# Nine convolution projections of a delta-rule stage as three products of rounded parts, with the weights' rests formed by GpSimd

## The chip, the cores and the metric

The kernel runs on one core of a Trainium2 chip. The metric is the device time of one execution in microseconds; the median of several runs counts. TensorE (PE) multiplies; ScalarE (ACT), VectorE (DVE) and GpSimd (POOL) work elementwise; SyncE (SP) issues nearly all loads.

## The reference

256 tokens of width 1024 go through two stacks of two layers each. The change lies at the seam: the first stack's last residual is normalised, normalised again for the second stack and modulated, and goes into the "gated delta rule" mixer:

```python
h = rmsnorm(x, norm_mix) * (1 + scale) + shift          # [256, 1024], float32
mixed, z, beta_in, a_in, q, k, v = split(h @ hy_w_in)    # first 1536 columns: mixed
mixed = causal_conv_silu(mixed, gdn_conv)                # 4 taps over tokens, then silu
```

The first 1536 columns of the product are twelve tiles of 128 channels, called `("conv", 0)` to `("conv", 11)` in the kernel. Their convolution gives the delta rule's query, key and value. The squares of the first eight tiles are summed per head (l2 norm), and a decay comes from eight further columns, the tile `("ba",)`. After it come four `z` tiles and twelve tiles `mq`, `mk`, `mv` of a second attention.

## The kernel before

Each projection tile is one "unit" of weights, 128x1024 float32 (512 KB), loaded by SP into one of eight slots of `ring` in a fixed order; a slot is loaded again when the unit that used it is done (`unit_done`). Activations are kept turned, channels on partitions, as eight blocks of 128x256 (`hT`, `xT`). PE writes tile t into PSUM bank t mod 3, and may start a tile only when the tile three before it has been evacuated (`evac`).

There are two ways of multiplying. `stream` (line 856) is a plain float32 product, eight matmuls of 256 columns for a unit. `stream_split` (line 878) takes operands rounded to the type float32r: it needs `weight_high` (a rounded copy of the weights in the arena, by ACT, `weights_high`, L1999), `weight_low` (the rest, weights minus rounded weights, written over the slot of the ring, by DVE, `weights_low`, L3054), and the same two parts of the activations (ACT, `rounded_hidden`, L1986; DVE, `split_hidden`, L3067). A unit is then 24 matmuls: rest of weights by rounded activations, rounded weights by rest of activations, rounded by rounded. Before the change the MLP, the first tiles of the first stack and the `pq` tiles of the second go this way; the convolution tiles don't.

`weights_high(label, ahead)` makes the rounded copies up to `ahead` units beyond the label, three unless told otherwise. There are four buffers (`HIGH = 4`), so the copy for a unit waits until the split unit four before it is done.

No engine is reordered at run time: each has its queue as the program writes it. Around the change the queues are these.

- PE: the last `down` tiles (split), the raw tiles `conv` 0 to 2 (L967, made from unnormalised activations), sums for a modulation vector (L1028), then `stream` of `conv` 3 to 11 (L856), `ba` (L852), sums of squares (L1514), four `z` and two `mq` tiles (L856), and then matmuls that wait for DVE (L1520).
- DVE: `two_norms` (the normalisation, `raw_out` of `conv` 0, the scaled activations L2640, `raw_out` of `conv` 1 and 2, a second reciprocal, the rescaling of `xT` L2690), a reduction of the modulation (L3031), and then in `gdn` for each of the twelve tiles one multiply and three multiply-adds (L3106, L3109), four taps of the convolution; after them the small decay operations, four operations L3136 and a large reciprocal (L2628).
- ACT: the root (L1810), the shift of `hT` (L1798), the second root, and then in `gdn` the loop below.
- POOL: idle until the shifted `hT` is there, and then two small loads (L2437) of the decay's inputs into `ab_t`, which lay inside the area of `weight_high`.

The loop on ACT, where `silu(j)` first waits for DVE's taps of tile j:

```python
for j in range(12):
    if j < RAW:                  # RAW = 3; DVE has evacuated these
        by_vector(("conv", j))
    else:
        evac(("conv", j), conv_in[:, j, 3:3 + S])
    if j >= 2:
        silu(j - 2)
```

Of the kernel before, what the change touches and what calls it, by code (L numbers as in the profile page):

```python
# [27 lines left out]
P = 128  # L28
S = 256
# [146 lines left out]
def two_stacks(nc, io, out):  # L176
    ctx = ExitStack()
    with ctx:
# [14 lines left out]
        def rounded(name, over, first, shape):  # L193

            t = nc.alloc_sbuf_tensor_at(name, shape, F32R, offset=address[over] + 4 * first)
            return t[(slice(None),) * len(shape)]
# [173 lines left out]
                tile(("sub", l, j), [unit_of(sk[4 * j:4 * j + 4].rearrange("a n d -> n a d"), P, 4, P)], P)  # L370
            stage_units[l] = len(units)

        IN_PARTS = ("up", "down", "sk", "sr", "sv", "pc", "pq")
        PLAIN = {kind: [(l, j) for l in range(DEPTH) for j in range(RAW)] for kind in ("pq", "up")}
        gate_units, narrow = [], {}
        for l in range(DEPTH):
            for b in (0, 3, 1):
# [23 lines left out]

        def last_in_parts(label):

            for kinds in (("sk", "sr", "sv", "pc"), ("up", "down"), ("pq",)):
                if label[0] in kinds:
                    return [x for x in tiles if x[0] in kinds and x[1] == label[1]][-1]
# [119 lines left out]
        hidden_high = rounded("hidden_high", "arena", 25856, [P, KD, S])  # L526
        first_weight_high = rounded("first_weight_high", "arena", 0, [P, HIGH, 1024])
        first_high, first_low = rounded("first_high", "uT", 0, [P, KD, S]), rounded("first_low", "arena", 30112, [P, KD, S])
        second_low = rounded("second_low", "arena", 27904, [P, KD, S])
        early_high, early_low = rounded("early_high", "arena", 21760, [P, EARLY_SLOTS, 1024]), rounded("early_low", "ring", 2 * 1024, [P, EARLY_SLOTS + 1, 1024])  # L530
        LOW_AT = (0, 1, 3)
# [39 lines left out]
        beta_t = area(W0 + 7208, TT, 4)  # L571
        sp_t = area(W0 + 7216, 3, TT, 4)
        eg_t = area(W0 + 7240, 3, TT, 4)
        ab_t = area(W0 + 7264, 1, 8)

        lat = area(2048, 6, S)
        lat_sq = area(3584, 6, S)
# [249 lines left out]
        def _(eng):  # L827
# [862 lines left out]
            for l in range(DEPTH):  # L1690
                norms[0] += 1
                if l == 0:
                    for j in range(RAW, 12):
                        stream(("conv", j), hidden)
                    stream(("ba",), hidden, tokens=True)
                    gdn(l, iter(gdn_fill()))
                    begun = mix_begun(l)
                else:
                    raw_columns([("c", j) for j in range(RAW)], raw_c, 3)
                    for j in range(RAW, 6):  # L1700
                        stream(("c", j), hidden)
                        for k in {3: (0, 1, 2), 4: (3,), 5: ()}[j]:
                            square_sum(lat_sq, k, 4)
                    stream(("kr",), hidden)
                    for k in range(2):
                        square_sum(lat_sq[:, 4:6, :], k, 2, 5)
                    turns = mla_rope()
                    ropes = pe.uses["rope_done"]
                    for j in range(4):
                        stream(("qr", j), latent)  # L1710
                        rotate(turns[j], j)
                    project(("qn", 0))
                    rotate(turns[4], 4)
                    for name in ("kn", "lv"):
                        project((name, 0))
                    eng.wait_ge(sem("kr_ready"), pe.next("kr_ready"))
                    attention(mla_jobs(ropes), mla_fill())
                    begun = []

                def mix(m):  # L1720
                    if m < len(begun):
                        mix_ended(*begun[m])
                    else:
                        stream(("mix", l, m), lambda i: mix_t[:, i, :])

                to_residual(mix, last=0)
                norms[0] += 1
                raw_tiles([("pq", l, j) for j in range(RAW)], raw_pq, S + 1, lambda k: square_sum(square, k, KD))
                experts(l)
                gate_matrices(l)  # L1730
                expert_tiles(l)
# [11 lines left out]
        def _(eng):  # L1743
# [280 lines left out]
            def gdn(fill):  # L2024
# [14 lines left out]
                for j in range(12):  # L2039
                    if j < RAW:  # L2040
                        by_vector(("conv", j))
                    else:
                        evac(("conv", j), conv_in[:, j, 3:3 + S])
                    if j >= 2:
                        silu(j - 2)
# [212 lines left out]
            for l in range(DEPTH):  # L2258
                root(rstd)
                if l == 0:  # L2260
                    eng.wait_ge(sem("vec_ready"), act.next("vec_ready"))
                    eng.activation(cond, vec[:, 3, VEC3["c"][0]:VEC3["c"][0] + 8], ACT.Silu).then_inc(sem("vec_ready"), 1)
                rounded_hidden(2 * l, first_high)
                weights_high(("sk", l, 0), 1)
                for label in first_tiles(l):
                    if in_parts(label):
                        weights_high(label)
                    if l == 0 and label in FIRST_SINES:
                        sines(FIRST_SINES.index(label))
                    if label == (LORA_IN[0], l, LORA_IN[1]):  # L2270
                        lora_inputs(l)
                    projected(label)
                lora(l)
                head_norms(l)
                for label in key_tiles(l):
                    projected(label)
                for label in rope_fill(l)[:2]:
                    projected(label)
                decays(l)
                for label in rope_fill(l)[2:] + indexer_fill(l):  # L2280
                    projected(label)
                attention(dsa_jobs(), attention_fill(l), lambda j: gates_ahead(l, j))
                fill = iter(rwkv_fill(l))
                retention(l, fill)
                rwkv(l, fill)
                for m in range(KD):
                    projected(("branch", l, m, 1))
                to_residual("wout", l, res_s, raw_up, vec[:, l, 8:16])
                root(rstd)
                rounded_hidden(2 * l + 1, hidden_high)  # L2290
                for j in range(DFF // P):
                    if l == 1 and j in SINES:
                        sines(SINES.index(j))
                    if j < RAW:
                        by_vector(("up", l, j))
                    else:
                        weights_high(("up", l, j))
                        evac(("up", l, j), up_t[:, j, :], ACT.Relu)
                    eng.wait_ge(sem("evac"), tiles[("up", l, j)][0] + 1)
                    eng.activation(up_t[:, j, :], up_t[:, j, :], ACT.Square).then_inc(sem("act_step"), 1)  # L2300
                    eng.wait_ge(sem("act_step"), act.next("act_step"))
                    eng.activation(up_high[:, j, :], up_t[:, j, :], ACT.Copy).then_inc(sem("up_high"), 1)
                if l == 0:
                    to_residual("down", l, res_s)
                else:
                    to_residual("down", l, res_s, raw_conv, gains_f, square_both)
            for l in range(DEPTH):
                if l == 0:
                    root(rstd, float(D))
# [2 lines left out]
                    root(rstd)  # L2312
                shifted_hidden(l, 0)
                if l == 0:
                    root(rstd2)
                    gdn(iter(gdn_fill()))
                else:
                    for j in range(6):
                        if j < RAW:
                            by_vector(("c", j))  # L2320
                        else:
                            evac(("c", j), lat[:, j, :])
                        eng.wait_ge(sem("evac"), tiles[("c", j)][0] + 1)
                        square_of(j, lat, lat_sq)
                    evac(("kr",), kr_t[:, 0, :])
                    root(rstd)
                    root(rstd)
                    for j in range(4):
                        evac(("qr", j), qr_t[:, j, :])
                    for name in ("qn", "kn", "lv"):  # L2330
                        projected((name, 0))
                    attention(mla_jobs(), mla_fill())
# [16 lines left out]
        def _(eng):  # L2349
# [68 lines left out]
            for l in range(DEPTH):  # L2418
# [13 lines left out]
                        ALU.subtract).then_inc(sem("g_low"), 1)  # L2432
                for b in (0, 3):
                    gated(l, b)
            eng.wait_ge(sem("h_ready"), 5 * KD)
            for i, name in enumerate(("gdn_a_log_2", "gdn_dt_bias_2")):
                eng.dma_start(ab_t[:, 0, 4 * i:4 * i + 4], io[name].to_broadcast([P, 4])).then_inc(sem("decay_in"), 16)  # L2437
# [153 lines left out]
        def _(eng):  # L2591
# [83 lines left out]
            def two_norms():  # L2675
# [9 lines left out]
                shifted_later(gains_f)  # L2685
                for j in range(1, RAW):
                    raw_out(("conv", j), conv_in[:, j, 3:3 + S])
                root(rstd2)
                for k in range(KD):
                    ins = stt_(xT[:, k, :], xT[:, k, :], vec[:, 3, fg + k:fg + k + 1], rstd2, ALU.mult, ALU.mult)  # L2690
# [844 lines left out]
```

## Time and profile before

| | |
|---|---|
| median of 3 runs | 3479.36 us (3476.62 to 3481.10) |
| the profiled execution | 3475.42 us, span 3473.6 us |
| PE busy | 3393.0 us, 98% |
| DVE busy | 2452.4 us, 71% |
| ACT busy | 1631.6 us, 47% |
| POOL busy | 323.6 us, 9% |
| shares of the chain that ended last | PE 88%, DVE 7%, ACT 2% |

Busy time is an average over many stages. The chain that ended last is followed back from the last instruction, at each step to what released it, so it tells which engine set the time of a stage.

### The profile page before, as it was taken

Reading aid. Unit: us, or ns where it says so; the run is one execution under the profiler, and the core shown is the slowest. Engines: PE = TensorE matmul, PEld = TensorE weight load, DVE = VectorE, ACT = ScalarE, POOL = GpSimd, SP = SyncE. Lnnn points to the kernel's source line nnn. Section 1 sums busy time; section 2 is a strip of 40 time slices with the busy share of each in tenths; the row PEclk is TensorE's granted clock in tenths of the full one; section 3 lists DMA queues with packets and bytes.
Section 4 is the critical chain, followed back from the end, with each engine's and each line's share of the span. In section 5 each row is a group of like instructions: output and inputs, shape, how many; then the busy total and the mean of one; then the engine's idle time right before and its main releaser. Section 6 shows DMA issues by size and latency. Waiting matters only on the chain.

```text
span 3473.6 us, 69683 instructions
## 1 busy us (share of the span) xinstructions
PE 3393.0 (98%) x24714; PEld 3070.1 (88%) x24714; DVE 2452.4 (71%) x5105; ACT 1631.6 (47%) x3275; POOL 323.6 (9%) x438
## 2 busy tenths in 40 slices
PE   8999999999999999999999999999999999999998
PEld 7879899988888998889988888888889888888887
DVE  6734457665434866537998888888538998888887
ACT  5153355433423743235555555555445555555554
POOL 0212000020210000000370000000000550000000
PEclk9999999999999999989999999999999999999999
DMA  8633378864335976234337887777444258787875
GB/s 231 177 90 94 110 220 268 239 178 136 87 93 155 270 233 162 62 88 138 111 101 195 196 196 191 197 195 186 106 132 151 84 135 195 193 194 194 195 195 135
DMA packets 644022, 565.20 MB, mean 163 GB/s; under 512 B 62027, under 2 KB 589402, under 8 KB 643546
## 3 DMA queue, kind: packets, MB, share of 16 engines
q1 hardware_dynamic: 638564, 542.16, 59.1%
q0 software_dynamic: 4960, 19.93, 1.7%
q8 instruction: 149, 2.44, 0.3%
q14 instruction: 71, 0.58, 0.1%
q10 hardware_dynamic: 278, 0.08, 0.0%
HBM read 550.52 MB, written 9.44 MB: 161 GB/s over the span
## 4 chain that ended last, share of the span: by engine, by line
PE 88%; DVE 7%; ACT 2%; issue 1%; DMA 1%; SPq 0%; POOL 0%; DVEq 0%; ACTq 0%; POOLq 0%
PE bank L1461 15%; PE bank L878 15%; PE bank L856 14%; PE bank L1481 7%; PE bank L1475 7%; PE bank L1478 7%; PE bank L899 4%; PE bank L1411 3%; PE bank L1436 2%; PE bank L852 2%; DVE uT L3331 2%; PE bank L1390 1%; PE bank L1270 1%; PE bank L967 1%; PE bank L1421 1%
## 5 line engine op out<-in xcount | busy, mean ns | idle before, releaser
L1461 PE MATMUL bank<-t_high,u_parts 128*128 128x256 f32 x3072 | 424.8, 280 | 1.3 <-ACT u_parts L2200 1.3
L1461 PEld LDWEIGHTS bank<-t_high,u_parts 128*128 128x128 f32 x3072 | 403.2, 188 | 20.9 <-ACT u_parts L2200 3.0
L3370 DVE TENSOR_TENSOR v_low<-ring,v_high 128x512 fp32r<-128x512 f32 x512 | 337.0, 690 | 59.7 <-ACT v_high L2212 35.4
L1481 PE MATMUL bank<-v_low,w_high 128*128 128x512 f32 x1024 | 323.1, 397 | 0.0
L1475 PE MATMUL bank<-v_high,w_high 128*128 128x512 f32 x1024 | 318.8, 392 | 0.9 <-ACT v_high L2212 0.9
L2212 ACT ACTIVATE v_high<-ring 128x512 fp32r<-128x512 f32 x512 | 299.2, 620 | 38.3 <-PE bank L1481 38.2
L1478 PE MATMUL bank<-v_high,w_low 128*128 128x512 f32 x1024 | 316.1, 390 | 0.0
L2415 POOL TENSOR_SCALAR uT<-cst,selT 128x128 f32<-128x128 f32 x256 | 188.2, 744 | 1312.7 <-ACT selT L2137 1308.4
L2200 ACT ACTIVATE u_parts<-bank 128x512 fp32r<-128x512 f32 x384 | 219.9, 594 | 191.3 <-DVE bank L3342 188.3
L1764 ACT ACTIVATE arena<-bank 128x256 f32<-128x256 f32 (+1 forms) x270 | 103.8, 387 | 437.7 <-PE bank L856 242.2
L856 PE MATMUL bank<-hT,ring 128*128 128x256 f32 (+2 forms) x1232 | 277.6, 382 | 8.3 <-DVE hT L2640 6.1
L856 PE MATMUL bank<-arena,ring 128*128 128x256 f32 (+2 forms) x1168 | 272.4, 385 | 5.7 <-DVE arena L3076 3.0
L856 PEld LDWEIGHTS bank<-hT,ring 128*128 128x128 f32 (+2 forms) x1232 | 228.3, 187 | 49.2 <-issue 15.0
L3349 DVE TENSOR_TENSOR u_parts<-bank,u_parts 128x512 fp32r<-128x512 f32 x384 | 247.2, 685 | 10.6 <-ACT u_parts L2200 0.4
L856 PEld LDWEIGHTS bank<-arena,ring 128*128 128x128 f32 (+2 forms) x1168 | 217.6, 191 | 40.9 <-DVE arena L3076 3.9
L3342 DVE STREAM_TRANSPOSE bank<-ring 128x512 f32<-128x512 f32 x384 | 252.0, 702 | 0.3 <-DMA ring<-in_peer_u 0.3
L2223 ACT ACTIVATE w_high<-tab 128x256 fp32r<-128x256 f32 x256 | 107.1, 418 | 283.5 <-DVE tab L3364 281.8
L1478 PEld LDWEIGHTS bank<-v_high,w_low 128*128 128x128 f32 x1024 | 192.3, 188 | 42.8
L1481 PEld LDWEIGHTS bank<-v_low,w_high 128*128 128x128 f32 x1024 | 192.1, 188 | 40.9 <-DVE v_low L3370 0.2
L1461 PE MATMUL bank<-t_low,u_parts 128*128 128x256 f32 x1536 | 214.7, 281 | 0.6
L3054 DVE TENSOR_TENSOR weight_low<-ring,weight_high 128x1024 fp32r<-128x1024 f32 x148 | 179.7, 1221 | 41.3 <-ACT weight_high L1999 40.5
L1475 PEld LDWEIGHTS bank<-v_high,w_high 128*128 128x128 f32 x1024 | 178.8, 188 | 31.7 <-ACT w_high L2223 1.7
(467 smaller groups left out, 6423.7 us busy)
## 6 DMA issues: line engine op xcount, KB each, us to landing
ring<-in_peer_v SPq DMA_DIRECT2D x256, 512.0 KB, 4.5
ring<-in_peer_u SPq DMA_DIRECT2D x768, 128.0 KB, 4.3
ring<-in_w_in SPq DMA_DIRECT2D x128, 512.0 KB, 4.1
ring<-in_mlp_up SPq DMA_DIRECT2D x64, 512.0 KB, 4.2
uT<-in_mod_w SPq DMA_DIRECT2D x64, 512.0 KB, 5.1
ring<-in_mlp_down SPq DMA_DIRECT2D x64, 512.0 KB, 4.4
ring<-in_peer_u SPq DMA_DIRECT2D x64, 512.0 KB, 3.8
arena<-in_mod_w POOLq DMA_DIRECT2D x32, 512.0 KB, 4.9
```

The source lines that it names most:

```text
L856: ins = eng.matmul(ps[0:n, 0:width], wv[:, i, :], moving(u * 8 + i), start=(u == 0 and i == 0), stop=(u == count - 1 and i == k - 1))
L878: ins = eng.matmul(PB[t % BANKS][:, 0:S], w[:, i, :], x[:, u * 8 + i, :], start=(u == 0 and part == 0 and i == 0), stop=(u == count - 1 an ...
L1461: ins = eng.matmul(PB[6 + b][:, 0:S], u_parts[:, part, k * P:k * P + P], moving[:, k, :], start=(n == 0), stop=(n == len(products) - 1))
L1475: eng.matmul(PB[2 * tt + q][:, :], w_high[:, b, t], v_high[:, d], start=first, stop=False)
L1478: eng.matmul(PB[2 * tt + q][:, :], w_low[:, b, t], v_high[:, d], start=False, stop=False)
L1481: ins = eng.matmul(PB[2 * tt + q][:, :], w_high[:, b, t], v_low[:, j % 4, d], start=False, stop=last)
L2200: eng.activation(u_parts[:, 0, d], PB[4 + q][:, :], ACT.Copy).then_inc(sem("uH_ready"), 1)
L2212: eng.activation(v_high[:, d], ring[:, 2 + j % 4, d], ACT.Copy).then_inc(sem("vH_ready"), 1)
L2415: ins = ts_(one_p[:, b, j, :], C("iota"), selT[:, 1, at], None, ALU.is_equal)
L3342: eng.transpose(PB[4 + q][:, :].rearrange("p (k e j) -> p k e j", e=QUADS, j=32), blocks_of(f, q)).then_inc(sem("u_turned"), 1)
L3349: tt_(u_parts[:, 1, d], PB[4 + q][:, :], u_parts[:, 0, d].bitcast(F32), ALU.subtract).then_inc(sem("uL_ready"), 1)
L3370: tt_(v_low[:, j % 4, d], ring[:, 2 + j % 4, d], v_high[:, d].bitcast(F32), ALU.subtract).then_inc(sem("vL_ready"), 1)
```

## The change

`conv` 3 to 11 go through `stream_split`. The rounded parts of the weights come from ACT: two units (3 and 4) behind the last `down` tile, the others in the loop of `gdn`, in front of the evacuation of each tile. The rests of the nine units come from POOL, in a loop ahead of its two small loads. The activations are rounded by ACT behind the shift of `hT`, and their rest (`conv_low`) is formed by DVE in `two_norms`, between `raw_out` of `conv` 2 and the second reciprocal. `ab_t` moves out of the way of `weight_high`.

```diff
-        IN_PARTS = ("up", "down", "sk", "sr", "sv", "pc", "pq")
+        IN_PARTS = ("up", "down", "sk", "sr", "sv", "pc", "pq", "conv")
+        PLAIN["conv"] = [(j,) for j in range(RAW)]
...
+            if label[0] == "conv":
+                return ("conv", 11)
...
+        conv_low = rounded("conv_low", "arena", 16384, [P, KD, S])
...
-        ab_t = area(W0 + 7264, 1, 8)
+        ab_t = small[:, 96:104].unsqueeze(1)
...
                     for j in range(RAW, 12):
-                        stream(("conv", j), hidden)
+                        stream_split(("conv", j), hidden_high, conv_low,
+                                     ("hidden_high", "hidden_split") if j == RAW else (None, None))
...
                     else:
+                        weights_high(("conv", j))
                         evac(("conv", j), conv_in[:, j, 3:3 + S])
...
                     to_residual("down", l, res_s, raw_conv, gains_f, square_both)
+                    weights_high(("conv", RAW), 1)
...
                 shifted_hidden(l, 0)
                 if l == 0:
+                    rounded_hidden(2 * DEPTH, hidden_high)
                     root(rstd2)
...
+            for n in split_units[split_end(("conv", RAW)) - 1:split_end(("conv", 11))]:
+                eng.wait_ge(sem("weight_high"), split_at[n] + 1)
+                tt_(weight_low[:, slot_of[n], :], ring[:, slot_of[n], :], high_of(n).bitcast(F32),
+                    ALU.subtract).then_inc(sem("weight_low"), 1)
             eng.wait_ge(sem("h_ready"), 5 * KD)
...
                 for j in range(1, RAW):
                     raw_out(("conv", j), conv_in[:, j, 3:3 + S])
+                split_hidden(hidden_high, conv_low)
+                low_made[0] = split_end(("conv", 11))
                 root(rstd2)
```

## Rows read from the trace of the kernel before

**Rows 1.** The page: busy times, shares of the chain.

```profile
PE 3393.0 (98%) x24714; PEld 3070.1 (88%) x24714; DVE 2452.4 (71%) x5105; ACT 1631.6 (47%) x3275; POOL 323.6 (9%) x438
PE 88%; DVE 7%; ACT 2%; issue 1%; DMA 1%; SPq 0%; POOL 0%; DVEq 0%; ACTq 0%; POOLq 0%
```

**Rows 2.** The chain in order of time: start us, us, what.

```profile
1298.10 11.51 PE bank L878 x96
...
1323.52 31.11 PE bank L856 x144
...
1385.80 0.38 PE bank L1520 x2
```

**Rows 3.** Timeline of ACT and DVE: start us, us, instruction, idle before it.

```profile
1312.31 1.28 ACT L1810 ACT_TABLE_LOAD   x1
...
1316.76 0.42 ACT L1810 ACTIVATE selT<-selT 128x256 f32<-128x256 f32 x1 [3.16 <-DVE selT L2628]
...
1318.70 3.30 ACT L1798 ACTIVATE hT<-hT,mod 128x256 f32<-128x256 f32 x8 [1.52 <-DVE hT L2640]
...
1322.75 0.43 DVE L2664 TENSOR_TENSOR arena<-bank,selT 128x256 f32<-128x256 f32 x1 [0.40 <-PE bank L967]
...
1330.95 0.35 DVE L3106 TENSOR_SCALAR arena<-arena,vec 128x256 f32<-128x256 f32 x1
...
1332.90 0.42 ACT L2028 ACTIVATE arena<-arena 128x256 f32<-128x256 f32 x1 [5.73 <-DVE arena L3109]
...
1355.54 1.53 DVE L3109 SCALAR_TENSOR_TENSOR arena<-arena,vec 128x256 f32<-128x256 f32 x3
...
1358.21 0.71 ACT L2028 ACTIVATE arena<-arena 128x256 f32<-128x256 f32 x2
```

**Rows 4.** Groups by line and shape in 1322 to 1358 us.

```profile
L3109 DVE SCALAR_TENSOR_TENSOR arena<-arena,vec 128x256 f32<-128x256 f32 x36 | 17.4, 484 | 1.3
L3106 DVE TENSOR_SCALAR arena<-arena,vec 128x256 f32<-128x256 f32 x12 | 4.2, 354 | 3.2 <-ACT arena L1764 2.8
```

**Rows 5.** Single lines: durations ns min/median/max, first and last start.

```profile
L1999 ACT ACTIVATE weight_high<-ring x148: 1039/1047/1067, 465.1 to 2599.9; 128x1024 fp32r<-128x1024 f32 x148
L1986 ACT ACTIVATE hidden_high<-hT x32: 398/409/418, 476.0 to 2570.5; 128x256 fp32r<-128x256 f32 x32
L2431 POOL TENSOR_TENSOR g_low<-hT,g_high x8: 1264/1764/2332, 235.9 to 885.1; 128x512 fp32r<-128x512 f32 x8
L2368 POOL TENSOR_TENSOR arena<-arena,selT x32: 722/732/1062, 249.3 to 1030.4; 128x256 f32<-128x256 f32 x32
L3022 DVE SCALAR_TENSOR_TENSOR arena<-arena,cond x28: 1276/1284/1747, 41.3 to 762.4; 128x1024 f32<-128x1024 f32 x28
```

**Rows 6.** Groups by line and shape, whole span, DVE.

```profile
L3067 DVE TENSOR_TENSOR second_low<-hT,hidden_high 128x256 fp32r<-128x256 f32 x16 | 5.5, 419 | 0.1
```

**Rows 7.** Timeline of POOL and DVE, three places where both work.

```profile
117.29 0.64 POOL L2388 TENSOR_TENSOR arena<-arena 128x271 f32<-128x271 f32 x1
117.35 1.66 DVE L3022 SCALAR_TENSOR_TENSOR arena<-arena,cond 128x1024 f32<-128x1024 f32 x1 [3.00 <-DMA arena<-in_mod_w]
...
240.57 1.23 DVE L2807 TENSOR_TENSOR weight_low<-ring,gate_high 128x1024 fp32r<-128x1024 f32 x1 [1.06 <-ACT gate_high L1852]
240.60 2.33 POOL L2431 TENSOR_TENSOR g_low<-hT,g_high 128x512 fp32r<-128x512 f32 x1
...
772.25 2.99 POOL L2388 TENSOR_TENSOR arena<-arena 128x271 f32<-128x271 f32 x4
772.28 0.88 DVE L2714 TENSOR_TENSOR arena<-arena,tab 128x256 f32<-128x256 f32 x1
```

**Rows 8.** The load issued in 1307.8 to 1307.9 us: KB, us to landing.

```profile
ring<-in_hy_w_in SPq DMA_DIRECT2D x1, 512.0 KB, 7.0
```

**Rows 9.** Stretches: us, busy of PE, PEld, DVE, ACT, POOL, granted clock, DMA.

```profile
1358.20:1361.60 3.40, 3.40 (x9) 2.69 (x9) 0.57 (x4) 3.37 (x6) 0.00 (x0) 0.50 0.59 153
1361.60:1385.80 24.20, 22.46 (x104) 19.43 (x104) 18.44 (x11) 9.99 (x15) 0.00 (x0) 1.00 0.44 112
```

## The prediction

> **What bounds the kernel now.** I read the page first. PE is busy 98% of the span and stands for 88% of the chain that ended last [rows 1]. So time saved on PE counts at first sight, and DVE and POOL look as if they had room. That average decides nothing for a change that touches 60 us. I therefore read the chain in order of time from 1298 to 1386 us, the timeline of ACT and DVE there, and then every place in the trace where POOL and DVE work at once.
>
> The chain [rows 2] is PE for as long as it projects: 144 plain matmuls in 31.11 us from 1323.52 (nine tiles of convolution and no wait among them, 3.457 us a tile), then the narrow ones for `ba`. Then it leaves PE: ACT and DVE do the decay and a large reciprocal, and PE's matmuls L1520 start at 1385.80 because DVE let them. So what matters for the rest of the kernel is the moment when the last silu lets this tail begin. That silu is the second of the pair that starts at 1358.21, and the pair waits for the evacuation of `ba`. DVE's last tap ends at 1355.54 + 1.53 = 1357.07 [rows 3], so DVE has only about 1.4 us in hand at that point.
>
> DVE starts its taps at 1330.95. A tile is one multiply of 0.354 and three multiply-adds of 0.484 us [rows 4], 1.95 us with the gaps, 23.4 us for twelve. From 1330.95 to 1357.07 are 26.1 us, so DVE waited for tiles in only 2.8 of them (the idle time ahead of L3106 that ACT's evacuation ended [rows 4]). This stretch is balanced between PE and DVE. The reader should keep that: PE's share of 98% hides an engine that is full here as well.
>
> **Part 1, PE.** A split tile is 24 matmuls. 96 of them take 11.51 us in the `down` tiles [rows 2], 2.88 us for 24. Plain is 3.457. Nine tiles save 9 x 0.577 = 5.2 us of PE, if PE is fed.
>
> **Part 2, the activations.** ACT rounds eight blocks of 0.409 us [rows 5] behind the shift, which ends at 1322.0 [rows 3]: done at about 1325.5. DVE's eight subtractions are 0.419 us each [rows 6], 3.4 us, and stand between `raw_out` of tile 2, which starts at 1322.75 [rows 3], and its second reciprocal. Everything behind moves by 3.4 us, and the taps start at 1334.35. Tile 3 on PE waits for these parts block by block and ends at about 1328.2, tile 4 at 1331.1.
>
> The first two roundings of weights stand ahead of ACT's root at 1316.76 [rows 3]. The load of tile 4 lands 7.0 us after its issue at about 1307.7 [rows 8], so its copy begins at 1314.7, ends at 1315.8, and the table for the root (1.28 us) is there at 1317.1, some 0.4 late. DVE idles 0.40 us ahead of `raw_out` of tile 2 at 1322.75 [rows 3], so I put it at nothing; without that cover it costs 0.4.
>
> **Part 3, where the weights' copies stand on ACT.** This is the first stop. The copies of tiles 5 and 6 are written in the iteration j = 3 of the loop, behind silu(0), and silu(0) waits for DVE's first tile. It ran at 1332.90 [rows 3] and would now run at 1336.35. Then come two copies of 1.05 us [rows 5] and POOL's rest of tile 5. PE, ready for tile 5 at 1331.1, starts it at about 1340.5: a gap of 9 us, more than the 5.2 it gains. From then on the copy for tile j+3 stands behind silu(j-3), so each further rest can only be made when DVE has finished one more tile.
>
> **Part 4, the rests on POOL.** The trace has no subtraction of 128x1024 on POOL. 256 columns take 0.722 and 512 take 1.264 at the least [rows 5], 2.1 ns a column, so 1024 take 1.264 + 512 x 0.0021 = 2.34 us; twice the 512 would be 2.53. POOL alone could feed a PE of 2.88 us a tile. But it isn't alone. At 240.57 and 240.60 DVE and POOL start, each on two operands in SBUF [rows 7]. DVE takes its 1.23 and ends at 241.80, POOL takes 2.33 in place of 1.26 and ends at 242.93, 1.13 after DVE. It stood still while DVE ran. The reverse is at 117.29: POOL is first, and DVE's L3022, started 0.06 later, takes 1.66 in place of 1.28, so it was held until 0.44 after POOL's start, with 0.20 of POOL's 0.64 left. At 772.28 a DVE operation of 0.42 takes 0.88 beside POOL [rows 7]. They take turns, and POOL gets its turn between two DVE instructions that follow closely.
>
> So a rest of 2.34 us keeps DVE out for 2.34 less 0.20 at its end (from 117.29) and 0.13 at its start (1.26 alone, 1.13 behind DVE), 2.0 us. Rests 3 and 4 fall at 1314 to 1318.8, where DVE reads PSUM or waits. The other seven fall among the taps, where DVE always has a next one to run: 7 x 2.0 = 14.0 us. Bounds: if what is held doesn't grow with the instruction, 7 x 0.46 = 3.2 us; if it is 2.53 us, 17.7. I take 14.0, since in rows 7 the hold follows the length of the instruction that has the turn, both ways round.
>
> The Trainium skill ("SBUF — State Buffer", section "SBUF: two separate sides") has it as a rule that speaks against this change: the port pair that the two engines share is an exclusive lock held for the whole instruction, and a VectorE operation with two SBUF inputs needs it against a GpSimd operation that reads SBUF. By that rule the seven rests would cost 7 x 2.34 = 16.4 us in place of 14.0. The trace agrees in kind, 1.66 for 1.28 us. "GPSIMD Engine Reference", section "Performance versus the Vector engine", gives 4497 ns for an addition of two operands of 2048 columns, from which an estimate for 1024 is 2.25 us.
>
> **The sum, at the tail's start.** DVE: 3.4 (start) + 14.0 (held) - 2.8 (its waits for tiles go, for it is now always behind) puts the end of the last tap at 1371.7, 14.6 later. Of this 1.4 is covered by the time in hand before silu(11): 13.2 us. PE isn't later than that: the rest of tile 11 follows silu(5), at about 1362, and PE would have `ba` done at 1368.3. POOL's two small loads now leave at about 1362 and have 9 us. PE's six fill tiles of 3.46 us behind `ba` end at about 1394, and L1520 can start at 1399.0, so 5 us of PE stand idle where 1.7 did (24.20 less 22.46 busy [rows 9]). Behind such a gap I expect the granted clock to be 0.5, the 1.2 GHz level, in one more stretch of 3.4 us, as it was at 1358.20 behind the narrow matmuls of `ba` [rows 9]; there PE had time to spare, behind 1399 it has not: 3.4 x 0.5 = 1.7 us. Sum: 13.2 + 1.7 = 14.9 us. Against the profiled execution that is 3475.4 + 14.9 = 3490.3; the median of before stands 3.9 us above that execution, so 3479.4 + 14.9 = 3494.3. Forecast 3494.
>
> **Rivals.** What this kernel's measurement can tell from no change is about 0.2%, 7 us, that is 3472.4 to 3486.3.
>
> (a) *POOL and DVE don't hold each other here.* Then DVE's taps would end at 1357.8, and PE would set the pace: tile 5 at 1340.5, seven tiles of 2.88 to 1360.7, `ba` at 1364.1 in place of 1358.1, the silus 5.9 us late: 3485, no change that can be measured. This is the case on the other side. Its place is the turns between L3109 and the new POOL line; it decides when the hold is below about 1.0 us per rest, for then 3.4 + 7 x 1.0 - 2.8 - 1.4 is no more than PE's 6. For it: the taps carry a scalar operand from SBUF and no row shows just such an instruction beside POOL. Against it: L3022, held by 0.38 us, is the same kind. A stretch at the low clock behind PE's gap of 9 us would add 1.7 and put it at 3487.
>
> (b) *The copies run ahead and PE is fed.* Then PE is done 3.4 us sooner than now, and DVE, 3.4 us later at its start and without waits, ends its taps at 1357.8, within the time in hand: 3479, no change. PE's 5.2 us would be lost on the tail. Only if the tail began sooner could it be faster, by 5 us at the very most. It needs ACT to copy tile 5 ahead of silu(0), against its order.
>
> (c) *The turns cost more.* Each rest held for 2.53 us, rests 3 and 4 colliding with the scaling L2640 (1 us), and PE at the low clock for two stretches: 14.9 + 3.7 + 1 + 1.7 = 21 us, 3501.
>
> **How the numbers follow.** My forecast with its clock stretch or without (3492.6) gets 0.70, (a) 0.14, half of it inside 7 us, (b) 0.06, (c) 0.10. The range from 3484 to 3501 leaves out (b) and part of (c). Slower 0.86, same 0.12, faster 0.02.
>
> **What would show it.** Right: a gap of PE of 9 us ahead of the sixth tile; POOL's subtraction of about 2.3 us, or up to 2.8 where it waits; in the taps single L3109 or L3106 of about 2.4 us, some seven of them; the last tap at about 1371.7; L1520 at about 1399. Wrong: taps that stay at 0.48 us (then (a)), no gap on PE (then (b)), or a stage behind 1400 us that regains time. What would upset it most is the hold per rest: 0.5 us on it is 3.5 us.

## The result, and the profile after

The changed kernel takes 3491.3 us (median of 6, 3487.32 to 3493.04) where the kernel before takes 3478.5 beside it: 1.0038 times as long, 95% interval 1.0028 to 1.0048, which is 13 us with 10 to 17 around it. That is well under 2%, but clear of no change. The forecast was 14.9 us more. The profiled execution has a span of 3485.5 us, 11.9 more than before.

In all that follows a stage is measured from VectorE's first operation on the sums of squares (1314.05 us before, 1312.53 after) to PE's first matmul behind its wait for VectorE (1385.80 before [rows 2], 1397.94 after). It was 71.75 us and is 85.41, 13.66 longer. That takes out what two executions differ in ahead of the stage. Here it is VectorE in the changed kernel, in order of time: start, duration, instruction.

```profile
1312.53 0.42 DVE L2691 TENSOR_SCALAR selT<-bank 128x256 f32<-128x256 f32 x1 [3.50 <-PE bank L941]
...
1322.33 2.77 DVE L3081 TENSOR_TENSOR conv_low<-hT,hidden_high 128x256 fp32r<-128x256 f32 x8
...
1332.30 0.35 DVE L3120 TENSOR_SCALAR arena<-arena,vec 128x256 f32<-128x256 f32 x1
1332.69 1.52 DVE L3123 SCALAR_TENSOR_TENSOR arena<-arena,vec 128x256 f32<-128x256 f32 x3
...
1338.35 2.35 DVE L3120 TENSOR_SCALAR arena<-arena,vec 128x256 f32<-128x256 f32 x1
...
1352.99 3.72 DVE L3123 SCALAR_TENSOR_TENSOR arena<-arena,vec 128x256 f32<-128x256 f32 x3
...
1369.09 1.53 DVE L3123 SCALAR_TENSOR_TENSOR arena<-arena,vec 128x256 f32<-128x256 f32 x3
```

The answers to [rows 3, 4] are here. Three multiply-adds take 1.52 us in the first tile and 3.72 in the sixth. The operations are the same; a wait inside an instruction counts as its busy time. No idle time stands ahead of any of them, so VectorE is never waiting for a tile, it is held. GpSimd at the same time:

```profile
1345.74 2.40 POOL L2445 TENSOR_TENSOR weight_low<-ring,weight_high 128x1024 fp32r<-128x1024 f32 x1 [2.80 <-ACT weight_high L2004]
1349.90 2.39 POOL L2445 TENSOR_TENSOR weight_low<-ring,weight_high 128x1024 fp32r<-128x1024 f32 x1 [1.76 <-ACT weight_high L2004]
1354.05 2.38 POOL L2445 TENSOR_TENSOR weight_low<-ring,weight_high 128x1024 fp32r<-128x1024 f32 x1 [1.76 <-ACT weight_high L2004]
```

One every 4.15 us, each behind a copy of ScalarE. The copies wait in turn: each stands behind the silu of an earlier tile, and that silu waits for VectorE's taps. So there is one rest for each tile of VectorE, and each tile is longer by the hold. PE, with its gap ahead of tile 5 and shorter ones later:

```profile
1328.26 1.12 PE L882 MATMUL bank<-hidden_high,weight_high 128*128 128x256 f32 x8
1338.18 2.05 PE L882 MATMUL bank<-hidden_high,weight_low 128*128 128x256 f32 x8 [8.80 <-POOL weight_low L2445]
...
1360.71 1.19 PE L882 MATMUL bank<-hidden_high,weight_low 128*128 128x256 f32 x8 [1.04 <-POOL weight_low L2445]
...
1397.94 0.59 PE L1524 MATMUL bank<-arena,cst 128*128 128x4 f32 x2 [3.02 <-DVE small L3158]
```

The chain that ended last, in order of time, has left PE in this stretch. Where [rows 2] had 31.11 us of PE there is now one tap after the other, the held ones with 2.7 us:

```profile
1353.51 0.50 DVE arena L3123
1354.04 2.69 DVE arena L3123
...
1357.13 0.50 DVE arena L3123
1357.66 0.50 DVE arena L3123
1358.18 2.69 DVE arena L3123
```

### The profile page after: what moved, and what is told of

The parts are those of the page before. It is cut to its first block, busy times and chain, and to the rows that moved or that the text cites. A ratio compares the mean times of both kernels' runs of the same rounds, so it can differ in the third digit from the quotient of the medians.

```text
span 3485.5 us, 69871 instructions
## 1 busy us (share of the span) xinstructions
PE 3394.0 (97%) x24786; PEld 3071.7 (88%) x24786; DVE 2471.7 (71%) x5113; ACT 1644.1 (47%) x3292; POOL 345.6 (10%) x447
## 4 chain that ended last, share of the span: by engine, by line
PE 86%; DVE 8%; ACT 2%; DMA 2%; issue 1%; SPq 1%; POOL 0%; DVEq 0%; ACTq 0%; POOLq 0%
PE bank L1465 15%; PE bank L882 15%; PE bank L860 13%; PE bank L1485 7%; PE bank L1479 7%; PE bank L1482 7%; PE bank L903 4%; PE bank L1415 3%; PE bank L1440 2%; PE bank L856 2%; DVE uT L3345 2%; PE bank L1394 1%; PE bank L1274 1%; DVE arena L3123 1%; PE bank L1425 1%
## 5 line engine op out<-in xcount | busy, mean ns | idle before, releaser
L860 PE MATMUL bank<-hT,ring 128*128 128x256 f32 (+2 forms) x1088 | 250.1, 386 | 6.4 <-DVE hT L2652 6.1
L860 PEld LDWEIGHTS bank<-hT,ring 128*128 128x128 f32 (+2 forms) x1088 | 203.2, 189 | 45.0 <-issue 13.3
```

Source lines behind the costliest of these rows:

```text
L860: ins = eng.matmul(ps[0:n, 0:width], wv[:, i, :], moving(u * 8 + i), start=(u == 0 and i == 0), stop=(u == count - 1 and i == k - 1))
```

## The experiments

All stages below are measured as above, on the run's own profile.

| kernel | taps from, to (us after the stage's start) | stage | ratio to the kernel before, 95% interval |
|---|---|---|---|
| before | 16.9, 43.0 | 71.8 | 1 |
| changed | 19.8, 58.1 | 85.4 | 1.0038 (1.0028 to 1.0048) |
| zeros in place of the rest | 19.6, 49.5 | 78.3 | 1.0022 (1.0012 to 1.0031) |
| copy in place of the rest | 19.6, 48.4 | 77.2 | one execution only, 3481.2 us |
| rest in four pieces | 20.3, 53.8 | 82.6 | 1.0035 (1.0021 to 1.0049) |
| early copies | 22.2, 56.5 | 83.8 | 1.0048 (1.0031 to 1.0065) |
| rests by VectorE | 21.9, 53.2 | 80.5 | 1.0030 (1.0020 to 1.0041) |
| late rescaling | 16.7, 55.0 | 82.4 | 1.0039 (1.0026 to 1.0053) |
| before, late rescaling | 13.6, 43.0 | 71.7 | 1.0004 (0.9994 to 1.0013) |
| early, late, by VectorE | 18.6, 49.9 | 77.3 | 1.0026 (1.0016 to 1.0036) |
| before, GpSimd beside it | 16.9, 54.7 | 82.0 | 1.0033 (1.0021 to 1.0044) |

The ratios don't follow the stages closely: the early copies have a shorter stage than the changed kernel and a larger ratio. What lies between the stage's end and the end of the kernel is the same work in all versions, and takes 2084.6 to 2095.3 us in the eleven profiles. Steps of a few microseconds between versions are therefore read from the stages, one profile each, and the ratios only tell each version from the kernel before.

### The cost by itself: GpSimd beside the kernel before

```diff
-            eng.wait_ge(sem("h_ready"), 5 * KD)
+            for j in range(RAW, 10):
+                eng.wait_ge(sem("evac"), tiles["conv", j][0] + 1)
+                tt_(arena[:, 21760:22784], cst[:, 0:1024], cst[:, 1024:2048], ALU.subtract).then_inc(sem("pool_step"), 1)
+                eng.wait_ge(sem("pool_step"), pool.next("pool_step"))
```

> The kernel before, plain products and all, with seven subtractions of 128x1024 on GpSimd whose result nobody uses, each let go by the evacuation of one of the tiles 3 to 9; nothing is left out. Only the cost beside VectorE is added. Theory 1: 7 x 2.13 = 14.9 us of holding, of which 2.8 (VectorE's waits for tiles) and 1.4 (time in hand before the last silu) are covered, so the stage goes from 71.8 to about 82.5 us and the kernel is some 10 us slower. Rival (the time comes from the copies, the gap or the split product): it stays at 71.8 us.

(The lines stand in GpSimd's queue, in place of the wait for `h_ready`; the two small loads follow.) The stage is 82.0 us, and the whole kernel 1.0033 times as long. Nothing here is split or copied; seven subtractions that nobody needs bring 10.3 of the 13.7 us. VectorE and GpSimd in this kernel:

```profile
1354.46 0.35 DVE L3109 TENSOR_SCALAR arena<-arena,vec 128x256 f32<-128x256 f32 x1
1354.85 3.59 DVE L3112 SCALAR_TENSOR_TENSOR arena<-arena,vec 128x256 f32<-128x256 f32 x3
```

```profile
1355.29 2.35 POOL L2437 TENSOR_TENSOR arena<-cst 128x1024 f32<-128x1024 f32 x1 [1.67 <-ACT arena L1764]
```

Three multiply-adds of 1.52 take 3.59: one subtraction of 2.35 us costs VectorE 2.07. The rival, that the time comes from the copies, the gap or the product, is left with 3.4 us, and these have owners too: the taps of the changed kernel start 2.9 us later, and its seven holds sum to 14.9 us in place of 14.4. The end of the last tap lies 27.32 us ahead of the stage's end in both kernels.

### What on GpSimd holds VectorE: zeros, and a copy

```diff
-                tt_(weight_low[:, slot_of[n], :], ring[:, slot_of[n], :], high_of(n).bitcast(F32),
-                    ALU.subtract).then_inc(sem("weight_low"), 1)
+                eng.memset(weight_low[:, slot_of[n], :].bitcast(F32), 0.0).then_inc(sem("weight_low"), 1)
```

> GpSimd writes zeros over the nine rests, with one memset of 1024 columns each, in place of the subtraction: the product of the weights' rests with the activations is zero, so that part is left out. The instruction is about as wide but reads nothing from SBUF. If it is the reading of two operands that keeps VectorE out, the multiply-adds stay at 0.48 us and the result is that of the short subtraction, about 3483 us. If any GpSimd instruction that uses SBUF keeps VectorE out, each costs its own length less 0.3 us (a memset of 64 columns takes 0.15 us, so 1024 perhaps 0.9 us): 7 x 0.6 = 4 us more than the short one, about 3487 us.

The "short subtraction" is a version in which GpSimd was to subtract only 16 of the 1024 columns. No time was taken of it; by its expectation the stage would have ended 8 to 10 us sooner if GpSimd's long instruction holds VectorE, and at most 2.3 us sooner if PE's gap is the cause.

```diff
+                eng.tensor_copy(weight_low[:, slot_of[n], :], high_of(n).bitcast(F32)).then_inc(sem("weight_low"), 1)
```

> GpSimd copies the rounded weights into the place of the rest, with one source of 1024 columns in place of two, so the rests are left out. It reads from SBUF, as the memset did not. If a read of SBUF by GpSimd is what holds the multiply-adds, they are held by about the copy's length less 0.3 us, tiles of some 3 us in place of 1.95; if it takes two operands on GpSimd, they stay at 0.48 us as beside the memset.

This version ran once, so no ratio is given for it; its trace is used for the length of single operations and for its stage.

Both GpSimd instructions are about equally long. First the memset (0.95 us) and VectorE beside it:

```profile
1338.59 1.99 POOL L2445 MEMSET weight_low<- 128x1024 f32 x2 [20.17 <-ACT weight_high L2004]
```

```profile
1339.12 0.56 DVE L3119 TENSOR_SCALAR arena<-arena,vec 128x256 f32<-128x256 f32 x1
1339.72 1.52 DVE L3122 SCALAR_TENSOR_TENSOR arena<-arena,vec 128x256 f32<-128x256 f32 x3
1341.28 0.87 DVE L3119 TENSOR_SCALAR arena<-arena,vec 128x256 f32<-128x256 f32 x1
```

The multiply-adds stay at 1.52 or 1.53 for three throughout. The multiply, with one tensor as its input, does not: 0.56 and 0.87 in place of 0.35. Now the copy (1.04 us):

```profile
1344.33 1.04 POOL L2445 CAST weight_low<-weight_high 128x1024 fp32r<-128x1024 f32 x1 [1.74 <-ACT weight_high L2004]
```

```profile
1343.29 2.35 DVE L3122 SCALAR_TENSOR_TENSOR arena<-arena,vec 128x256 f32<-128x256 f32 x3
```

Here three multiply-adds take 2.35, held for 0.83 us by an instruction of 1.04. So it isn't the number of operands on GpSimd, and not the writing: what holds an operation of VectorE with two operands from SBUF is a GpSimd instruction that reads SBUF, for its own length less 0.2 to 0.3 us (0.83 of 1.04, 2.07 of 2.35).

By the Trainium skill ("SBUF — State Buffer", section "SBUF: two separate sides"), two SBUF inputs collide only with a GpSimd operation that reads SBUF, and an operation in the two-port mode collides with any; it lists a multiply of this kind, `tensor_scalar`, among those that can run in that mode. The multiply-adds of these two kernels agree with the first half (1.52 beside the memset, 2.35 beside the copy). The multiply fits the second (0.87 beside the memset), but no view here shows in which mode it runs.

The zeros' kernel also measures my rival (a). VectorE's long waits are gone, PE still has 7.38 us of gap ahead of tile 5 and sets the pace; the stage is 78.3, 6.5 longer than before, where the rival gave 6. That the two agree is in part luck. Tile 5 starts 24.1 us after the stage's start, 2.3 sooner than the rival had it, above all because a memset is 1.4 us shorter than a subtraction. From there to `ba` PE takes 22.8 us in place of 20.2, because of a stretch at the 1.2 GHz level that the 6 us leave out; the rival named it apart, at 1.7 us:

```profile
1335.30:1345.50 10.20, 5.82 (x27) 5.85 (x28) 9.52 (x20) 5.78 (x11) 3.89 (x4) 0.50 0.00 0
```

(The stretch, its length, busy time and instructions of PE, PEld, VectorE, ScalarE and GpSimd, the granted clock, DMA's share and GB/s.) So without the hold the change would cost 6.5 us with a rest of 0.95 us, and by my estimate some 8 with one of 2.4, half of its 13.7 or a little more. The copy's kernel, whose PE had the low clock for a shorter time behind its gap, has the shorter stage of the two although its multiply-adds are held; its end is PE's as well.

### Turns: the rest in four pieces

```diff
+                for at in range(0, 1024, 256):
+                    c = slice(at, at + 256)
+                    ins = tt_(weight_low[:, slot_of[n], c], ring[:, slot_of[n], c], high_of(n)[:, c].bitcast(F32),
+                              ALU.subtract)
+                ins.then_inc(sem("weight_low"), 1)
```

> Each of the nine rests is formed by four GpSimd subtractions of 256 columns in place of one of 1024; nothing is left out. If VectorE is kept out for the whole of the one GpSimd instruction that runs, it now gets a turn between the pieces: single taps last at most about 0.9 us in place of 2.5, each rest costs VectorE 4 x 0.4 = 1.6 us in place of 2.13, the seven 3.7 us less, about 3488 us. If the two merely share a bandwidth, the tiles stay at 4.15 us and the time at 3491 us.

The taps of this kernel, to be held against the 0.35 and 3.72 of the changed one:

```profile
1349.78 0.71 DVE L3123 TENSOR_SCALAR arena<-arena,vec 128x256 f32<-128x256 f32 x1
1350.52 2.61 DVE L3126 SCALAR_TENSOR_TENSOR arena<-arena,vec 128x256 f32<-128x256 f32 x3
```

Every tap now waits about 0.36 us, none waits 2.2. From the first to the last tap are 33.5 us in place of 38.3, so a rest costs (33.5 - 23.4) / 7 = 1.45 us, less than the expected 1.6. The stage shrank by only 2.8, not 3.7. The taps start 0.5 us later, and they end 28.8 us ahead of the stage's end, 1.5 more than in the changed kernel: PE sets the end here. Its narrow matmuls of `ba` take 4.68 us in place of 3.63, at a granted clock of 0.76, and ScalarE's last silus stand behind their evacuation, which is this row:

```profile
1366.55 0.18 ACT L1769 ACTIVATE arena<-bank 128x16 f32<-128x16 f32 x1 [3.83 <-PE bank L856]
```

Sharing of a bandwidth is refuted: the tiles take 3.4 us, not 4.15. On the whole kernel the difference is too small to be seen.

### Is it PE's gap? Early copies

```diff
                     rounded_hidden(2 * DEPTH, hidden_high)
+                    weights_high(("conv", RAW))
                     root(rstd2)
```

> ScalarE rounds the weights of tiles 5 and 6 behind the rounding of the activations, ahead of its second root, so not behind the first silu; nothing is left out. PE's gap of 8.8 us ahead of tile 5 should go. Theory 1 (VectorE, held by GpSimd, sets the end): only the two rests that move from the taps to the reciprocal and the rescaling ahead of them can help, 2 to 4 us; about 3488 us. Rival (the gap sets the end): 8 to 9 us, about 3483 us.

The gap ahead of tile 5 is gone, but PE now waits 4.95 us ahead of tile 6, for the evacuation of tile 3, which stands behind a silu. Its first wait for a rest has 0.61 us:

```profile
1336.24 2.08 PE L882 MATMUL bank<-hidden_high,weight_low 128*128 128x256 f32 x8 [4.95 <-ACT arena L1769]
...
1345.55 1.19 PE L882 MATMUL bank<-hidden_high,weight_low 128*128 128x256 f32 x8 [0.61 <-POOL weight_low L2446]
...
1395.17 0.59 PE L1524 MATMUL bank<-arena,cst 128*128 128x4 f32 x2 [6.36 <-DVE small L3159]
```

The stage is 83.8 us, only 1.6 shorter, and PE waits 6.36 us at its end in place of 3.02. The idle time of PE that the two timelines show in the stage is 15.0 us in place of 14.4: it moved and did not shrink, so the gap was a symptom. This version alone is a weak test of it, as a gap of 4.95 us stands one tile later; the kernel with GpSimd beside it, which has none, is what rules the gap out. I had expected 2 to 4 us. The taps start 2.4 us later than in the changed kernel (22.2 against 19.8), since two rests now hold the rescaling, and last 4.0 us less, since only five hold the taps: 1.6 are left.

### Is VectorE the bound? The rescaling moved, in both kernels

Eight operations leave `two_norms`, and stand behind the taps, where VectorE waits for ScalarE's tables:

```diff
                 ts_(sp_t[:, 2, :, :], sp_t[:, 0, :, :], 0.0, None, ALU.max).then_inc(sem("act_in"), 1)
                 eng.wait_ge(sem("act_in"), dve.next("act_in"))
+                for k in range(KD):
+                    ins = stt_(xT[:, k, :], xT[:, k, :], vec[:, 3, fg + k:fg + k + 1], rstd2, ALU.mult, ALU.mult)
```

> The changed kernel with VectorE's rescaling of xT (eight operations, 3.3 us) moved from ahead of the taps to its idle time behind them, where it waits for ScalarE's tables; nothing is left out. If VectorE's queue sets the end of the stage, the stage shrinks by 3.3 us, 85.4 to 82.1. If PE's gap or the rests' rate on GpSimd sets it, nothing changes.

> The kernel before with the same rescaling moved; nothing is left out. There PE sets the end of the taps, so the 3.3 us that VectorE gains are idle time and the stage stays at 71.8 us, within 0.3. If VectorE already sets the end before the change, it would shrink towards 68.5.

The changed kernel's stage shrinks by 3.05 us, the other's by 0.04. The same edit is worth nearly all of its time (3.25 us) in the one and nothing in the other: before, PE set the end of the taps, and now VectorE does. For the whole of the changed kernel the 3 us don't show in the ratio, 1.0039 against 1.0038.

### The rests by VectorE itself

GpSimd's loop over the rests is taken out, and VectorE forms them:

```diff
-                low_made[0] = split_end(("conv", 11))
+                weights_low(("conv", RAW), 1)
...
                 for j in range(12):
+                    if j >= 2:
+                        weights_low(("conv", max(j, RAW)), 2 if j == 2 else 3)
                     copied_out(("conv", j))
```

> VectorE forms the nine rests itself (1.22 us each), two behind the activations' rest and seven between the taps; GpSimd has only its two small loads. Nothing is left out. Theory 1: VectorE pays 9 x 1.22 = 11.0 us in place of the 14.9 us for which it was held, so from its first operation of the stage to PE's first matmul behind it are about 81.5 us, where the changed kernel takes 85.4 and the kernel before 71.8; some 4 us below the changed kernel, and still about 10 above the one before. Rival (the work is better off VectorE, since GpSimd is idle anyway): slower than the changed kernel.

80.5 us, 4.9 below the changed kernel, where I had expected 4. A rest lasts 1.22 us on VectorE and moves the taps by 1.13, since it overlaps with the next operation; it costs 2.1 if GpSimd does it beside VectorE. All three edits together:

> Early copies of the weights of tiles 5 and 6, the rests by VectorE and the late rescaling together, nothing left out: the best that I can make of the split product here. VectorE from the activations' rest to the last tap: 3.4 + 11.0 - 3.3 - 4.2 (idle time and time in hand of the kernel before) = 6.9 us more than before: stage about 78.5 us, some 7 us above the kernel before and 6 to 7 below the changed one. It would beat the kernel before only if the three gained more than they do one by one.

77.3 us, and 1.0026 times the kernel before: by its stage the best of the split versions that keep the whole computation, and still slower than the kernel without a split. PE saves at most 5.2 us here. VectorE pays 9 x 1.13 = 10.2 for the rests and 2.9 for the activations' part, and had 4.2 to give, 7.4 with the late rescaling; that makes 5.7 us, and 5.5 were measured. No version that beats the kernel before came out of this, and by that count I don't see one with nine tiles.

## Why the prediction was right, point by point

**The start.** Forecast 3.4 us later; the taps start 19.77 us after the stage's start in place of 16.90, so 2.9. Eight subtractions that follow closely take 2.77, not 8 x 0.419: the durations overlap. That the two early copies stand ahead of the root cost nothing, as said: it ran 2.77 us after the stage's start in place of 2.71. Rest 3 and 4 held one operation of VectorE for half a microsecond, which I had left out.

**Part 3, the gap.** Forecast a gap of 9 us ahead of tile 5 (9.4 by the times it is worked out from), measured 8.80. That it costs nothing as long as VectorE is held was implied by the sum, and the added subtractions in the kernel before showed it: 82.0 us for the stage, with no wait of PE above 0.3 us among the tiles.

**Part 4, the hold.** GpSimd's subtraction was forecast at 2.34 us and takes 2.33 to 2.40. The hold was forecast at 7 x 2.0 = 14.0; from the first tap to the last are 38.3 us, less 23.4 is 14.9, so 2.13 each. The rule of the Trainium skill's page "SBUF — State Buffer" (section "SBUF: two separate sides"), taken for the whole length of the instruction, would have given 7 x 2.34 = 16.4 and was further off. Added up with what was measured, 2.9 + 14.9 - 2.8 - 1.4 = 13.6; the stage is 13.66 longer. The forecast was 13.2.

**The clock.** This is the term that was mis-sized. I added 1.7 us for one stretch of 3.4 us at the 1.2 GHz level behind the wait at the end of the stage. Such a stretch came, twice as long: the granted clock was 0.50 from 1397.3 for 6.8 us, and from PE's L1524 to the transposes behind the next tile are 7.5 us in place of 4.5, so 3.0 us. But it was not lost for good. The view by stretches shows it, with the columns given above. First the changed kernel, the low stretch and then the time from the stage's end to the next normalisation:

```profile
1397.30:1404.10 6.80, 6.16 (x19) 5.26 (x20) 2.73 (x13) 0.00 (x0) 0.00 (x0) 0.50 0.14 43
1397.94:1549.05 151.11, 145.17 (x1183) 125.67 (x1184) 65.03 (x186) 39.05 (x102) 0.00 (x0) 0.92 0.23 65
```

The same work in the kernel before:

```profile
1385.80:1540.34 154.54, 148.73 (x1183) 128.73 (x1184) 65.03 (x185) 38.98 (x102) 0.00 (x0) 0.90 0.23 66
```

In spite of the stretch at 0.50 the changed kernel was granted more over this work, 0.92 against 0.90, and did it in 3.4 us less; by the end of the kernel that lead is gone again, 2087.6 against 2087.8. The low stretches fall differently from profile to profile with the same work: the eleven profiles take 151.1 to 157.5 us for it, and the two ends of that range are the changed kernel and the one with GpSimd beside it. Nor does the stretch behind the stage follow PE's wait at its end. The changed kernel with late rescaling waits the same 3.02 us there and is granted 1.00 behind it; the kernel before with late rescaling waits the same 1.74 us as the kernel before and is granted 0.54 in the 7.5 us behind it. So nothing here shows the 1.7 us as a price of the change. Without them the forecast would have been 13.2, and 12.8 was measured. The interval of 10 to 17 holds 14.9 as well, so the whole kernel's time doesn't decide on this term; the stages and the profiles behind them do.

A second size was off: I had PE stand idle for 5 us at the end of the stage, and it did for 3.0. In part that is because `ba` and the sums of squares behind it took 10.4 us in place of 8.7, at a granted clock of 0.67 in place of 0.80. As VectorE sets the end of the stage, that cost nothing.

**The rivals.** (a), no hold, would have been 6 us; the zeros' kernel came out near it for that case, in part by luck as told above; but the hold is there. (b) fell with the gap. (c) didn't happen: rests 3 and 4 cost half a microsecond, not 1, and a turn was 2.1, not 2.5.

Of the absolute forecast, 3494, another 0.9 us is the kernel before, which took 3478.5 us beside the changed one and not 3479.4.

What stays open is why the clock's stretches lie as they do behind the stage; no run here was made for it.

## What to carry to other kernels

An idle GpSimd isn't free help for a busy VectorE. Before giving it elementwise work on SBUF, look at what VectorE does at the same time; if that is two-operand work, the price on VectorE is GpSimd's length less 0.2 to 0.3 us, here 2.1 us for a rest that VectorE forms itself in 1.22. The two lengths measured are 1.04 and some 2.4 us; for pieces of 256 columns the hold was 0.36 us. And where two engines are balanced, as PE and VectorE were in this stage, count the second one's time for an edit that relieves the first: PE's 5.2 us could not be had for 18 us on VectorE.

## What the runs showed of the hardware that I had not expected

A memset on GpSimd (0.95 us) leaves VectorE's multiply-adds alone and holds its one-operand multiply (0.35 to 0.87 us), while a copy of the same width (1.04 us) holds the multiply-adds for 0.83. I had not thought that the kind of either instruction would decide so sharply. And cutting GpSimd's instruction into four makes it longer in sum, 23.5 us for seven rests in place of 7 x 2.38 = 16.7, but cheaper for its neighbour, 1.45 us in place of 2.13.
